# Layer norms without GpSimd, function tables loaded early, and a stage's first two weight chunks multiplied in step

## The reference

```python
def layer_norm(x):
    xf = x.astype(jnp.float32)
    mu = jnp.mean(xf, axis=-1, keepdims=True)
    var = jnp.mean(jnp.square(xf - mu), axis=-1, keepdims=True)
    return ((xf - mu) * lax.rsqrt(var + EPS)).astype(x.dtype)
def modulate(x, shift, scale):
    return x * (1.0 + scale) + shift
def post_norm(x, y):
    return layer_norm(ALPHA * x + y)
def swiglu(h, w_in, w_out):
    gate, up = jnp.split(h @ w_in, 2, axis=-1)
    return (jax.nn.silu(gate) * up) @ w_out
def gla_out(o, r, norm_g):
    B, T = o.shape[:2]
    return rms_norm(o, norm_g).reshape(B, T, GLA_V) * jax.nn.silu(r)
```

## Time and profile before

| | us |
|---|---|
| median of 3 runs | 2435.7 (2434.52 to 2437.32) |
| the profiled execution | 2434.04 |
| its span, first to last instruction | 2431.5 |
| TensorE busy, mean granted clock | 2267.2 (93%), 0.972 |
| VectorE busy | 1470.1 (60%) |
| ScalarE busy | 977.4 (40%) |
| GpSimd busy | 819.0 (34%) |

### The profile page before, as it was taken

One profiled execution on the slowest core, in us unless ns is written; L12 is line 12 of the kernel. 1 busy time (PEld: TensorE's weight loads), 2 busy tenths in 40 slices (PEclk: granted clock), 3 DMA queues, 4 the chain that ended last, 5 costly groups with the idle time before them and its releaser, 6 DMA issues.

```text
span 2431.5 us, 32998 instructions
## 1 busy us (share of the span) xinstructions
PE 2267.2 (93%) x12738; PEld 1924.1 (79%) x12738; DVE 1470.1 (60%) x2100; ACT 977.4 (40%) x1580; POOL 819.0 (34%) x428
## 2 busy tenths in 40 slices
...
DMA packets 79544, 329.90 MB, mean 136 GB/s; under 512 B 18928, under 2 KB 29296, under 8 KB 55840
## 3 DMA queue, kind: packets, MB, share of 16 engines
...
## 4 chain that ended last, share of the span: by engine, by line
PE 80%; DVE 9%; ACT 5%; issue 3%; POOL 1%; DMA 0%; SPq 0%; DVEq 0%; POOLq 0%; ACTq 0%
PE ps L556 24%; PE ps L558 24%; PE ps L557 24%; PE ps L654 3%; PE ps L672 2%; DVE TMP L1587 2%; ACT WH L922 2%; PE ps L662 1%; DVE TMP L1634 1%; DVE WL L1391 1%; PE ps L769 1%; ACT L933 1%; DVE X L1696 1%; DMA WF<-in_w 0%; ACT L935 0%
## 5 line engine op out<-in xcount | busy, mean ns | idle before, releaser
L2014 POOL TENSOR_TENSOR WL<-WF,WH 128x1024 fp32r<-128x1024 f32 (+1 forms) x253 | 595.1, 2352 | 1328.2 <-ACT WH L922 1327.5
L556 PE MATMUL ps<-Hh,WH 128*128 128x256 f32 (+1 forms) x2526 | 873.1, 346 | 102.3 <-DVE Hl L1645 46.4
L557 PE MATMUL ps<-Hl,WH 128*128 128x256 f32 (+1 forms) x2526 | 865.5, 343 | 0.0
L558 PE MATMUL ps<-Hh,WL 128*128 128x256 f32 (+1 forms) x2526 | 864.9, 342 | 0.0
L556 PEld LDWEIGHTS ps<-Hh,WH 128*128 128x128 f32 x2526 | 488.9, 194 | 177.0 <-issue 100.1
L922 ACT CAST WH<-WF 128x1024 fp32r<-128x1024 f32 (+1 forms) x508 | 465.2, 955 | 266.6 <-PE ps L558 256.0
L558 PEld LDWEIGHTS ps<-Hh,WL 128*128 128x128 f32 x2526 | 488.4, 193 | 53.1
L557 PEld LDWEIGHTS ps<-Hl,WH 128*128 128x128 f32 x2526 | 489.3, 194 | 51.7 <-issue 0.2
L1471 DVE CUSTOM_DVE_ANT_0 TMP<-AR 128x1024 f32<-128x1024 f32 x216 | 414.1, 1956 | 23.4 <-DMA AR<-in_ada 22.3
L1391 DVE TENSOR_TENSOR WL<-WF,WH 128x1024 fp32r<-128x1024 f32 (+2 forms) x255 | 321.4, 1261 | 121.7 <-ACT WH L922 120.9
L556 PE MATMUL ps<-HIDh,WH 128*128 128x512 f32 (+1 forms) x880 | 307.3, 349 | 4.4 <-DVE WL L1391 3.6
...
## 6 DMA issues: line engine op xcount, KB each, us to landing
WF<-in_w SPq DMA_DIRECT2D x182, 1024.0 KB, 4.8
...
AR<-bias_rows SPq DMA_DIRECT2D x3, 1024.0 KB, 13.4
...
AR<-in_cond SPq DMA_DIRECT2D x2, 1024.0 KB, 6.9
...
X<-in_mem SPq DMA_DIRECT2D x1, 1024.0 KB, 14.8
```

The lines of the kernel that those rows point to most:

```text
L556: e.matmul(out, lh, rh, start=first, stop=False)
L557: e.matmul(out, lh, rl, start=False, stop=False)
L558: return e.matmul(out, ll, rh, start=False, stop=end)
L2014: e.tensor_tensor(l[:, k0:k1, :], src[:, k0:k1, :], h[:, k0:k1, :].bitcast(F32), ALU.subtract).then_inc(*up("p_lo", ("lo", i, 1)))
```

## The change

1. **Early tables.** `act_logs` and `act_silus` load the table of Ln, or of silu, ahead of need: at the start, before the output projections (wout, wo, eout, nout), at the entry of the feed-forwards and swiglus, and before their second down part. Exp behind Ln still loads its own. The silu of the GLA's gate moves from the eviction (L1232) to a block of four in place, behind the evictions of the value projection.
2. **Second chunk early.** The chunks in `SECOND` are converted ahead of the norm in front of their stage: half 0 before the square of tile 7, half 1 behind it (`act_last`). At the program's start the second chunk is converted directly behind the first, before Ln.
3. **Two chunks in step.** `pe_pair` multiplies a stage's first two chunks tile by tile of the activation, with up to four banks open.
4. **No GpSimd in the norm.** VectorE centres (`dve_centre`) and scales every tile, and tiles 1 to 7 go through ScalarE's scale and shift and a cast. GpSimd converts its half of the second chunk there; the product of the root by ALPHA comes at the end of `act_modulate`, and so do GpSimd's residuals behind it.

```diff
-        if n + 1 < len(WIDE) and WIDE[n + 1] - i <= 3:
+        if n + 1 < len(WIDE) and WIDE[n + 1] - i <= 3 and WIDE[n + 1] not in SECOND:
             out.append(WIDE[n + 1])
         return out
+
+
+
+    SECOND = {CH[name][j] for name, j in (("qa", 1), ("qm", 1), ("f0_gu", 1), ("f10_gu", 1), ("e_lr", 0), ("f20_gu", 1),
+                                          ("f11_gu", 1), ("n_q", 0), ("f21_gu", 1))}
+    AFTER = {"f10": CH["e_lr"][0], "mix0": CH["f20_gu"][1], "f20": CH["f11_gu"][1], "f11": CH["n_q"][0], "mix1": CH["f21_gu"][1],
+             "f21": None}
...
+    def pe_pair(e, of, *chunks):
+
+        outs = [[ps.take(e, t, *freed) for t, freed in tiles] for _, _, tiles in chunks]
+        n = nk(chunks[0][0])
+        kc = (n + 1) // 2
+        for k in range(n):
+            hi, lo, ready = of[k]
+            for (i, T, tiles), out in zip(chunks, outs):
+                h, l = parts_of(i)
+                if k in (0, kc):
+                    e.wait_ge(*at(("hi", i, int(k >= kc))))
+                    e.wait_ge(*at(("lo", i, int(k >= kc))))
+                if i == chunks[0][0]:
+                    for x in ready:
+                        e.wait_ge(*at(x))
+                for c, (t, _) in enumerate(tiles):
+                    col = slice(P * c, P * c + P)
+                    m = pe_product(e, out[c][:, 0:T], h[:, k, col], l[:, k, col], hi[:, 0:T], lo[:, 0:T], k == 0, k == n - 1)
+                    if k == n - 1:
+                        m.then_inc(*up("tile", ("done", t), *([("end", i)] if c == len(tiles) - 1 else [])))
+                    elif k == kc - 1 and c == len(tiles) - 1:
+                        m.then_inc(*up("half", ("half", i)))
...
     def pe_ffn(e, name, of, T, begun=None):
         for h in range(2):
-            for j in range(HALF):
+            if h == 0:
+                pe_pair(e, of, *[(CH[name + "_gu"][n], T, gate_tiles(name, n)) for n in range(2)])
+            for j in range(0 if h else 2, HALF):
                 n = HALF * h + j
-                i = CH[name + "_gu"][n]
-                pe_lin(e, i, of, T, [((name, "g", n), [(name, "ga", n)]), ((name, "u", n), [(name, "m", n)])], fresh=n == 0)
+                pe_lin(e, CH[name + "_gu"][n], of, T, gate_tiles(name, n))
             hid = [(HIDh[:, j, :], HIDl[:, j, :], [(name, "hidl", HALF * h + j)]) for j in range(HALF)]
...
-        pe_lin(e, CH["e_q"][0], of, T2, [(("gq", j), [("gq", j)]) for j in range(2)], fresh=True)
-        pe_lin(e, CH["e_lr"][0], of, T2, [(("lr", 0), [("lrt",), ("krd",)])])
+        pe_pair(e, of, (CH["e_q"][0], T2, [(("gq", j), [("gq", j)]) for j in range(2)]),
+                (CH["e_lr"][0], T2, [(("lr", 0), [("lrt",), ("krd",)])]))
...
+    def act_half(e, i, q):
+        src, (h, _) = staged(i), parts_of(i)
+        k0, k1 = halves(i)[q]
+        e.wait_ge(*at(("wf", i)))
+        if slot_freed(i, q):
+            e.wait_ge(*at(slot_freed(i, q)))
+        e.copy(h[:, k0:k1, :], src[:, k0:k1, :]).then_inc(*up("w_hi", ("hi", i, q)))
+
+    def act_logs(e):
+        e.preload_act_table_set("natural_log")
+
+    def act_silus(e):
+        e.preload_act_table_set("silu_and_others")
...
+            if h:
+                act_logs(e)
...
+    def act_last(e, st, T):
+
+        i = AFTER[st]
+        if i:
+            act_half(e, i, 0)
+        act_collect(e, st, 7, T)
+        if i and len(halves(i)) > 1:
+            act_half(e, i, 1)
+        act_norm(e, st, T)
...
-        e.wait_ge(*at((st, "root")))
-        e.mul(SQ[:, 0:T], r, ALPHA).then_inc(*up("mean", (st, "up")))
-
-    def act_modulate(e, st, l, g, T):
+
+    def act_modulate(e, st, before, l, g, T):
         e.wait_ge(*at(("mod", l, g)))
         for k in range(KT):
             t = TMP[k % 3]
             for r in range(T // S):
                 c = slice(S * r, S * r + S)
                 up_, sh = MOD[:, l, 8 * (g + 1) + k, r:r + 1], MOD[:, l, 8 * g + k, r:r + 1]
-                e.wait_ge(*at((st, "mt", k, 0 if k % 2 else r)))
-                if k % 2:
+                e.wait_ge(*at((st, "mt", k, 0 if k else r)))
+                if k:
                     e.activation(t[:, c], t[:, c], ACT.Identity, bias=sh, scale=up_).then_inc(*up("mod_t", (st, "mt2", k, r)))
                 else:
                     e.activation(Hh[:, k, c], t[:, c], ACT.Identity, bias=sh).then_inc(
                         *up("h_hi", (st, "mh", k, r), *([(st + "h", k)] if r == T // S - 1 else [])))
-            if k % 2:
+            if k:
                 e.wait_ge(*at((st, "mt2", k, T // S - 1)))
                 e.copy(Hh[:, k, 0:T], t[:, 0:T]).then_inc(*up("h_hi", (st + "h", k)))
+        e.mul(SQ[:, 0:T], STAT[0][:, 0:T], ALPHA).then_inc(*up("mean", (before, "up")))
...
     def act_swiglu(e, st, T, end=False):
+        act_silus(e)
         for h in range(2):
...
-                e.wait_ge(*at(("done", ("gr", c))))
-                e.activation(GR[:, c, :], ps["gr", c], ACT.Silu).then_inc(*up("a_evict", ("gr", c)))
+                act_evict(e, GR[:, c, :], ("gr", c)).then_inc(*up("a_evict", ("gr", c)))
...
+        act_silus(e)
+        for c in range(4):
+            e.wait_ge(*at(("gr", c)))
+            e.activation(GR[:, c, :], GR[:, c, :], ACT.Silu).then_inc(*up("silu", ("grs", c)))
...
         act_split(e, WIDE[0])
+        act_split(e, WIDE[1])
         e.wait_ge(*at(("const",)))
...
         act_highs(e, range(4, 8), {k: HT[k - 4] for k in range(4, 8)}, "yh", "yt")
+        act_logs(e)
         for c in range(4):
             act_splits(e, CH["wout"][c])
             for j in (2 * c, 2 * c + 1):
+                if j == 7:
+                    act_half(e, CH["qm"][1], 0)
                 act_square(e, HT[j], X[:, j, lat], ("wsq", j), ("wx", j))
+        act_half(e, CH["qm"][1], 1)
         act_root(e, "cross", S, D, 0)
         act_highs(e, range(KT), [HT[8 + k % 6] for k in range(KT)], "ch0", "ct")
...
+    def dve_centre(e, before, k, T):
+        e.wait_ge(*at((before, "xsq", k)))
+        e.tensor_tensor(X[:, k, 0:T], X[:, k, 0:T], SUM[:, 0:T], ALU.subtract).then_inc(*up("x", (before, "x_mu", k)))
+
     def dve_modulate(e, st, before, l, g, T):
 
         root = STAT[0]
-        e.wait_ge(*at((before, "root")))
         e.wait_ge(*at(("mod", l, g)))
         for k in range(KT + 1):
-            if k < KT and k % 2 == 0:
+            if k < KT:
                 t = TMP[k % 3]
+                if k > 1:
+                    dve_centre(e, before, k, T)
                 e.wait_ge(*at((before, "x_mu", k)))
                 if k >= 3:
                     e.wait_ge(*at((st + "l", k - 3)))
+                if k:
+                    e.tensor_tensor(t[:, 0:T], X[:, k, 0:T], root[:, 0:T], ALU.mult).then_inc(*up("scaled", (st, "mt", k, 0)))
+                else:
+                    e.wait_ge(*at((before, "root")))
+                    for r in range(T // S):
+                        c = slice(S * r, S * r + S)
+                        e.scalar_tensor_tensor(out=t[:, c], in0=X[:, k, c], scalar=MOD[:, l, 8 * (g + 1) + k, r:r + 1],
+                                               in1=root[:, c], op0=ALU.mult, op1=ALU.mult).then_inc(*up("scaled", (st, "mt", k, r)))
+            if k == 1:
                 for r in range(T // S):
                     c = slice(S * r, S * r + S)
-                    e.scalar_tensor_tensor(out=t[:, c], in0=X[:, k, c], scalar=MOD[:, l, 8 * (g + 1) + k, r:r + 1], in1=root[:, c],
-                                           op0=ALU.mult, op1=ALU.mult).then_inc(*up("scaled", (st, "mt", k, r)))
-            if k:
+                    e.wait_ge(*at((st, "mh", 0, r)))
+                    e.scalar_tensor_tensor(out=Hl[:, 0, c], in0=TMP[0][:, c], scalar=MOD[:, l, 8 * g, r:r + 1],
+                                           in1=Hh[:, 0, c].bitcast(F32), op0=ALU.add, op1=ALU.subtract).then_inc(
+                        *up("h_lo", *([(st + "l", 0)] if r == T // S - 1 else [])))
+            elif k:
                 i = k - 1
-                t = TMP[i % 3]
-                if i % 2:
-                    dve_low(e, Hl[:, i, 0:T], t[:, 0:T], Hh[:, i, 0:T], (st + "h", i), (st + "l", i))
-                else:
-                    for r in range(T // S):
-                        c = slice(S * r, S * r + S)
-                        e.wait_ge(*at((st, "mh", i, r)))
-                        e.scalar_tensor_tensor(out=Hl[:, i, c], in0=t[:, c], scalar=MOD[:, l, 8 * g + i, r:r + 1],
-                                               in1=Hh[:, i, c].bitcast(F32), op0=ALU.add, op1=ALU.subtract).then_inc(
-                            *up("h_lo", *([(st + "l", i)] if r == T // S - 1 else [])))
+                dve_low(e, Hl[:, i, 0:T], TMP[i % 3][:, 0:T], Hh[:, i, 0:T], (st + "h", i), (st + "l", i))
...
     def dve_end_norm(e, st, T):
+        if AFTER[st]:
+            dve_split(e, AFTER[st])
+        t = TMP[4][:, 0:T]
         e.wait_ge(*at((st, "musq")))
         e.wait_ge(*at((st, "m2")))
```

(59 more changed lines are left out.)

57 lines of the change are left out of this document (36 added, 21 removed).

## The result

The changed kernel takes 2452.5 us (2452.4 to 2453.4, 4 runs), the kernel before 2436.5 in the same comparison: a ratio of 1.0067, 95% interval 1.005 to 1.0085. It is slower by 16 us; 2451 was forecast. The profiled execution has a span of 2450.7 us against 2431.5, so by the spans, on which the forecast of +16.2 was built, it is +19.2: the execution that was profiled before took 2434.0 us, less than any of those behind the median. By the profile's page, TensorE is busy for 2281.0 us (before 2267.2), GpSimd for 755.9 (819.0).

A forecast was written before the change was run, and what follows sets the result against it. TensorE, 80% of the chain, was taken as the bound, so only its waits could change; the terms by place summed to +16.2 us on 2434.04, 2450.2, so a median of about 2451, 8-in-10 range 2438 to 2460.

The forecast's parts named there:

- Norm: Four large norms: without GpSimd's work and with the table load moved ahead, TensorE starts 4.1 us earlier in each.
- Third chunk's wait: Behind a pair, the third chunk's conversion stands behind output 0's silu and cast, so TensorE waits 2.4 us.
- Start, wout, down part, end: Second chunk's early conversion +2.9; table loads before wanted casts +1.3 and +1.3; VectorE centring six tiles at the end +1.5.
- Cross: Cross stage, +3.6 us: lead +0.45 from new casts before Ln, third chunk's wait 1.85, slow clock 1.3.
- Silus: Silus of the gate, +3.5 us: a table load and four activations now stand before casts that TensorE waits for.
- Ffn: First feed-forward, +4.7 us: its loop starts only at the pair's first output, moving later turns by 4.4; lead 0.3.
- f20, f11: Second and third swiglu, -5.5 and -0.9 us: earlier starts and tile pace against 3.9 us lost behind each pair.
- TensorE waits 2.4 us, and its clock then falls: Behind pairs: half speed after the third chunk's wait costs another 1.3 to 1.5 us, 3.9 in all per stall.
- the first rival: The clock doesn't fall behind stalls of 2 us: 7.1 us go, giving +9.1, 2444 us; chance 0.14.
- odd mixer: Odd mixer, -0.4 us: -4.1 from its start and -0.8 of tile pace, against 3.9 behind the pair.
- even mixer: Even mixer, -2.1 us: start 4.1 earlier, but the next chunk's conversion joins the chain with 2.2 to 3.3 us.
- The rival of contention in the pair: VectorE too busy: pairs wait 0.3 us a tile in five stages of 512 columns, 12 more, 2463 us; chance 0.05.

The follow-up runs named there:

- run 1: The changed kernel, with the third chunk's first half converted before output 0's silu or eviction in six stages: 2441.8 us.
- run 2: The changed kernel with the two chunks of each pair multiplied one after the other: 2430.2 us.
- run 3: The changed kernel with the gate's silus at their eviction, no early table loads at wout and second f0_dn, and the old start without its pair: 2444.1 us.
- run 8: On top of run 1, first halves of e_k and n_v converted early and the low-rank copy ahead of e_k's second cast: 2437.2 us.

## Why the prediction was right

Its number was right, and the mechanism of most of its terms, but one step was wrong, and that its error was made up for elsewhere is luck. By the stretches of the table above, the forecast's terms and what the profiled execution has:

| | to wout | to ffn | to 2nd half | to f10 | to mix0 | mix0 to f20 | to f11 | to mix1 | mix1 to f21 | to end |
|---|---|---|---|---|---|---|---|---|---|---|
| forecast | +4.2 | +3.9 | +4.4 | +1.8 | -0.2 | +1.4 | -5.5 | -0.9 | +2.8 | +4.3 |
| measured | +4.9 | +1.2 | +3.9 | +3.1 | -1.1 | +4.8 | -5.6 | -1.1 | +4.9 | +4.3 |

- *Norm*: 4.1 us earlier forecast, 4.2 measured, in all four large ones.
- *Third chunk's wait*: 2.4 forecast, 2.44 measured; run 1 shows the cause, and run 2 the price of pairing as a whole, 22 us, which the sum didn't state as one.
- *Start, wout, down part, end*: 2.9, 1.3, 1.3, 1.5 forecast; 1.6 (3.4 by the product at 173.06, at 169.63 before), 1.5, 1.4, 1.2 measured.
- *Cross*: 3.6 forecast, and 3.9 with the lead of the feed-forward; 1.2 measured. The norm waits 3.92 instead of 4.25, where I had it start 0.45 later, the third chunk waits 1.68 for the 1.85 of the forecast, and the 1.3 of slow clock did not come.
- *Silus*: 3.5 forecast; the product that waits for their casts comes 2.9 later (1078.45), the whole rest of the mixer takes 4.8 longer, and 2.4 come back in run 3.
- *Ffn*: 4.4 of the loop forecast, 3.9 measured. The slow clock behind its 4.59 us is mostly made up at once, as the next two turns don't wait.
- *f20, f11*: -5.5 and -0.9 forecast, -5.6 and -1.1 measured, but with other parts: the 1.5 of clock behind the third chunk did not come, the pair took 24.1 us (1247.03 to 1271.14) and not 23.2, and the fourth chunk came 0.5 later still.
- The step that failed is "TensorE waits 2.4 us, and its clock then falls". It stayed at 1.00 behind the third chunks' waits of 1.7 to 2.6 us (the rows at 570.50 and 1273.60 above). That took 7.1 us out of the sum, as the first rival said, which would have made 2444.
- What filled the gap are pauses that I had not priced: the pair gives n_v no cover, so it waits 3.78 us for GpSimd, and the slow clock behind it costs 2.8 (odd mixer +6.0 up to its norm, 3.7 forecast); the copy of the low-rank product stands behind e_k's casts, so that TensorE waits 2.58 for it, with a clock of about 0.5 for the 10 us behind it (even mixer up to e_k +4.1, 2.0 forecast); 1.3 more of clock is lost between the value projection at 54.47 and the product at 173.06, and 1.6 behind the 2.15 us at 507.49. And a pair runs at half speed at a stage's start with nothing to hide it. The traces show all of these as sizes; only the first two were tested by an edit (run 8, and run 2 for n_v).

The rival of contention in the pair (VectorE too busy) did not happen: from 918.60 to 924.00, at half speed, TensorE is busy for 5.35 of 5.40 us, and from 924.00 to 935.00, at full speed, for all 11.00.
